# Router logits on two column tiles, and the first expert block's rows gathered in the routing phase

## The reference, cut to what matters

```python
def hierarchical_moe(x, w_rg, b_rg, w_re, b_re, w1, w3, w2):
    p_group = jax.nn.softmax((xf @ w_rg).astype(jnp.float32) + b_rg, axis=-1)
    g_sel = jnp.argmax(p_group, axis=-1)
    e_logits = ((xf @ w_re).astype(jnp.float32) + b_re).reshape(T, N_GROUPS, EXPERTS_PER_GROUP)
    ...
    top_v, top_i = lax.top_k(e_in, TOP_K)
    gate = jax.nn.softmax(top_v, axis=-1) * jnp.take_along_axis(p_group, g_sel[:, None], axis=1)
    ...
    h = jax.nn.silu(lax.ragged_dot(xs, w1, sizes)) * lax.ragged_dot(xs, w3, sizes)
    o = lax.ragged_dot(h, w2, sizes) * gate_s[:, None].astype(x.dtype)
    y = jnp.zeros_like(xf).at[tok_s].add(o)
```

## Time and profile before

| | |
|---|---|
| median of 3 runs | 5463.49 us (5462.31 to 5465.83) |
| the profiled execution itself | 5458.19 us |
| its span | 5456.2 us |
| PE busy | 5086.9 us, 93% of the span |
| DVE busy | 3838.7 us, 70% |
| ACT busy | 2904.5 us, 53% |
| POOL busy | 1286.4 us, 24% |
| mean granted clock of PE | 0.965 |

### The profile page before, as it was taken

The page is one execution under the profiler, slowest core; times in us unless marked ns, Lnnn a source line. Parts: engine busy times, 40 slices in busy tenths (PEclk is TensorE's granted clock), DMA queues, the critical chain, the costliest instruction groups (busy, mean ns, idle before and its releaser), DMA issues. The chain is left out here.

```text
span 5456.2 us, 109973 instructions
## 1 busy us (share of the span) xinstructions
PE 5086.9 (93%) x36030; PEld 4377.2 (80%) x36031; DVE 3838.7 (70%) x6659; ACT 2904.5 (53%) x4913; POOL 1286.4 (24%) x1184
## 2 busy tenths in 40 slices
PE   8999999999999998979999959998999996999994
PEld 6989798988889986868888847888888785888883
DVE  6778887777666668686877747875444556866987
ACT  3343444344388886455756534443777213654765
POOL 2110020000011110054544432200100003543555
PEclk9999999999999998989999979999999997999997
DMA  6776765455499987588998856655545436987997
GB/s 217 216 209 202 207 211 167 125 153 142 140 317 312 316 287 209 162 318 272 330 329 277 282 185 215 224 159 170 166 143 160 131 128 220 326 261 238 364 326 254
DMA packets 755211, 1237.12 MB, mean 227 GB/s; under 512 B 111838, under 2 KB 407277, under 8 KB 754828
## 3 DMA queue, kind: packets, MB, share of 16 engines
q1 hardware_dynamic: 630108, 877.59, 49.4%
q0 software_dynamic: 75312, 286.28, 16.8%
q10 hardware_dynamic: 49408, 68.17, 3.7%
HBM read 917.08 MB, written 333.67 MB: 229 GB/s over the span
## 5 line engine op out<-in xcount | busy, mean ns | idle before, releaser
L622 PE MATMUL qa_ps_out<-qa_x_hi,qa_w_hi 128*128 128x512 f32 x1344 | 529.8, 394 | 23.2 <-DVE qa_w_lo L784 12.9
L622 PE MATMUL qa_ps_out<-qa_x_lo,qa_w_hi 128*128 128x512 f32 x1344 | 525.4, 391 | 0.0
L622 PE MATMUL qa_ps_out<-qa_x_hi,qa_w_lo 128*128 128x512 f32 x1344 | 525.3, 391 | 0.0
L668 ACT ACTIVATE qa_w_hi<-qa_w_whole 128x1024 fp32r<-128x1024 f32 x180 | 191.2, 1062 | 428.7 <-PE qa_ps_out L622 221.7
L622 PE MATMUL qa_ps_out<-qa_w_hi,qa_x_hi 128*128 128x256 f32 x1344 | 381.3, 284 | 0.0
L622 PE MATMUL qa_ps_out<-qa_w_hi,qa_x_lo 128*128 128x256 f32 x1344 | 380.3, 283 | 0.0
L622 PE MATMUL qa_ps_out<-qa_w_lo,qa_x_hi 128*128 128x256 f32 x1344 | 380.3, 283 | 0.0
L2895 DVE CUSTOM_DVE_ANT_0 ga_minus_s<-ga_ps_s,ga_bias 128x512 f32<-128x512 f32 (+1 forms) x256 | 185.4, 725 | 252.7 <-PE ga_ps_s L2831 200.1
L1336 ACT ACTIVATE da_prob<-da_minus_s,da_rows 128x256 f32<-128x256 f32 (+1 forms) x768 | 317.7, 464 | 41.3 <-DVE da_rows L1304 41.3
L1304 DVE CUSTOM_DVE_ANT_0 da_minus_s<-da_ps_s,da_bias 128x256 f32<-128x256 f32 (+1 forms) x768 | 259.9, 375 | 90.4 <-PE da_ps_s L1235 79.3
L622 PEld LDWEIGHTS qa_ps_out<-qa_x_hi,qa_w_hi 128*128 128x128 f32 x1344 | 253.9, 189 | 81.3 <-DVE qa_w_lo L784 17.5
(11 more groups left out here) (523 smaller groups left out, 15475.4 us busy)
## 6 DMA issues: line engine op xcount, KB each, us to landing
a_ex_w_raw<-w SPq DMA_DIRECT2D x128, 1024.0 KB, 8.6
b_ex_w_raw<-w SPq DMA_DIRECT2D x128, 1024.0 KB, 9.4
qa_w_raw<-w_qkv_a SPq DMA_DIRECT2D x144, 512.0 KB, 4.8
a_ex_w_raw<-w POOLq DMA_DIRECT2D x66, 1024.0 KB, 8.6
b_ex_w_raw<-w POOLq DMA_DIRECT2D x66, 1024.0 KB, 8.3
da_q_cross<-qT SPq DMA_DIRECT2D x48, 1024.0 KB, 7.7
da_k_parts<-kT SPq DMA_DIRECT2D x48, 1024.0 KB, 10.1
a_in_o<-o SPq DMA_DIRECT2D x16, 1584.0 KB, 8.0
```

What stands on the lines that cost most here:

```text
L622: done = pe.matmul(out, stationary, moving, start=(k == 0 and i == 0), stop=(k == KH - 1 and i == 2))
L668: act.activation(w_hi[:, p % W_RING], src, ACT.Copy).then_inc(w_hi_done, 1)
```

## The change

Four things change; the rest of the program is the same.
- The logits: `wr` is padded to 64 columns instead of 128, and each of the 8 steps becomes two matmuls, one for tokens 0 to 63 and one for tokens 64 to 127 of the tile, on two column tiles of the array (`tile_position`), writing the upper and the lower 64 partitions of ps_l.
- The first gather: x_row and its semaphore move to `ExpertWeights`, which lives through both phases, and POOL issues the gather of block 0 in the routing phase, after the second entry of its table, once DVE has written `tokens` (new semaphore tokens_kept). The remaining table entries come after it.
- DVE in the routing phase makes `tokens` between the two halves of gate_at; POOL issues the first loads of w2 at its beginning, after waiting for the last load of side 0.
- DVE in the experts phase makes the low part of piece 0 alone ahead of xT_lo, and of pieces 1 to 7 after it.

```diff
-        wr = sb("wr", [P, KC, P])
+        wr = sb("wr", [P, KC, HD])
...
-        ps_l = ps("ps_l", [P, P])
+        ps_l = ps("ps_l", [P, HD])
...
                     for k in range(KC):
-                        done = pe.matmul(ps_l[:], x1T[:, k, :], wr[:, k, :], start=(k == 0), stop=(k == KC - 1))
+                        for side in range(2):
+                            toks = bass.ts(side, HD)
+                            done = pe.matmul(ps_l[toks, :], x1T[:, k, toks], wr[:, k, :], start=(k == 0),
+                                             stop=(k == KC - 1), tile_position=(0, HD * side))
                     done.then_inc(routed, 1)
...
+        self.x_row = ctx.enter_context(nc.sbuf_tensor(f"{tag}_x_row", [P, D], F32))
+        self.x_loaded = sem("x_loaded")
...
                 link(pool.memset(pack[:], 0.0))
+                pool.wait_ge(weights.w13_loaded[W13_PIECES // 2 - 1], 32)
+                for i in range(W2_PIECES // 2):
+                    weights.load_w2(pool, 0, i).then_inc(weights.w2_loaded[i], 16)
                 pool.wait_ge(expert_copied, 1)
...
                 put(routing.PACK, pack[:])
                 put(routing.SIDE, expert_side[:, 1])
+                pool.wait_ge(tokens_kept, 1)
+                pool.indirect_dma_start(out=weights.x_row[:], out_offset=None, in_=scratch.x1,
+                                        in_offset=bass.IndirectOffsetOnAxis(ap=routing.tokens[:, 0:1], axis=0)
+                                        ).then_inc(weights.x_loaded, 16)
                 put(routing.FETCH, fetch[:])
...
-                pool.wait_ge(weights.w13_loaded[W13_PIECES // 2 - 1], 32)
-                for i in range(W2_PIECES // 2):
-                    weights.load_w2(pool, 0, i).then_inc(weights.w2_loaded[i], 16)
...
-                for h in range(2):
+                def mark_gates(h):
...
                 link(dve.memset(place[:, B:B + 1], 0.0))
+                mark_gates(0)
                 dve.wait_ge(inverted, 1)
...
-                link(dve.tensor_copy(routing.tokens[:], place[:]))
+                dve.tensor_copy(routing.tokens[:], place[:]).then_inc(tokens_kept, 1)
+                mark_gates(1)
                 dve.wait_ge(gates_placed, 1)
...
-                split_w13(dve, 0, at.count, 0, range(4), "lo")
+                split_w13(dve, 0, at.count, 0, range(1), "lo")
                 x_parts(0)
-                split_w13(dve, 0, at.count, 0, range(4, DVE_LOWS), "lo")
+                split_w13(dve, 0, at.count, 0, range(1, DVE_LOWS), "lo")
...
-                    if first(b):
-                        pool.indirect_dma_start(out=x_row[:], out_offset=None, in_=scratch.x1,
-                                                in_offset=bass.IndirectOffsetOnAxis(ap=routing.tokens[:, 0:1], axis=0)
-                                                ).then_inc(x_loaded, 16)
-                        pool.sem_inc(picked, 1)
-                        return
...
-                gather_x(0)
+                pool.sem_inc(picked, 1)
```

More of the change, by code:

```diff
@@ L1901, in route_tokens @@
         inverted, gates_marked, gates_placed = sem("inverted"), sem("gates_marked"), sem("gates_placed")
+        tokens_kept = sem("tokens_kept")
         logits = routing.logits
@@ L2300, in experts @@
         w_lo = sb("w_lo", [P, EXPERT_PIECES, D], F32R)
-        x_row = sb("x_row", [P, D])
+        x_row = weights.x_row
         column = sb("column", [P, 1], U32)
@@ L2320, in experts @@
         stepped = sem("stepped")
-        x_loaded = sem("x_loaded")
+        x_loaded = weights.x_loaded
         x_turned = sem("x_turned")
```

## The result

| | before | after |
|---|---|---|
| median | 5464.66 us (6 runs, 5460.20 to 5471.73) | 5433.79 us (6 runs, 5431.86 to 5442.25) |
| the profiled execution | 5458.19 us | 5432.38 us |
| its span | 5456.2 us | 5430.7 us |

The ratio of after to before is 0.9948, with a 95% interval of 0.9938 to 0.9958: some 28 us faster (23 to 34). The two medians are 30.9 us apart. So the sign and the places were right, and a part of the gain was not foreseen.

A forecast was written before the change was run, and what follows sets the result against it. PE, busy in 93% of the span, was taken to bound the kernel. Merges 14.4 us plus starts of the experts 6.6 made 21.0 us saved, forecasting 5442.5 us, with a range of 5434 to 5455.

The forecast's parts named there:

- The group, 1.18 us: PE's logit group in the merges: 32 records at the attention's 0.034 us plus 0.10 for changing tiling, 1.18 instead of 1.70.
- Merges, 14.4 us: Both merges save 14.4 us: 5.0 in layer a, 6.8 in layer b, and 1.3 at each end.
- The ends, 1.3 each: Last two logit groups of each merge: 1.3 us saved per layer, bounds 0.3 and 2.2; route(14) saves 1.2.
- The routing phase, 0.4 later: The routing phase ends 0.4 us later, as PE's ps_gates group must follow the delayed second half of gate_at.
- The start of the experts, 3.3 per layer: PE, freed from waiting for the gather, begins the experts phase 3.3 us earlier per layer, 6.6 in all; bounds 0 and 3.8.
- land within the phase either way: Routing phase: the w2 loads land within it either way and are used only in the next phase.
- covered, by 0.8 us: POOL in the routing phase ends by 2354.6, DVE at 2355.4, so POOL's added work stays hidden by 0.8 us.
- Rival C: More is saved: logit group halved without a tiling price, PE starts experts 3.8 us earlier; 27.1 saved, 5436.4 us; chance 0.14.
- A: Start of the experts does not move, held by PE's table reading or DVE's low parts; 14.4 saved, 5449.1 us; chance 0.14.
- B: In merge a the loop of load and DVE takes all of the 5.0 us; 16.0 saved, 5447.5 us; chance 0.10.
- D: The two tiles' logit matmuls don't run beside each other; group 1.89 us, 1 saved in all, 5462.4 us; chance 0.06.
- E: Slower: a logit record keeps 0.11 us, group 3.6 us in both merges; 54 us more, 5518 us; chance 0.03.

The follow-up runs named there:

- four tiles: The change with the logits on four column tiles of 32 tokens and 40 columns, 64 records in rotation: 5424.1 us, ratio to before 0.9929.
- Tiles in turn: The change with its 16 logit matmuls reordered, all 8 steps on the first column tile, then 8 on the second: 5454.2 us.
- w2 first: The kernel before with only POOL's first two loads of w2 moved to the beginning of the routing phase: 5460.1 us against 5465.8.
- logits alone: The kernel before with the router logits on two column tiles and nothing else: 5453.7 us against 5465.8, ratio 0.9975.

## Why the prediction was right, and where it fell short

- **The group, 1.18 us**: right, from the attention's row. The period of a tile in layer b fell by 0.49, forecast 0.52. By the rule of 60 cycles a matmul (the Trainium skill, TensorEngine Tiling (Array Packing), Instruction Overhead) the edit brings nothing. For tiles in rotation it does not hold: at 2.4 GHz 60 cycles are 0.025 us, and a record of four tiles takes 0.0114. Tiles in turn come out near the prediction's estimate from that page, 0.057 against 0.052, and there the edit indeed brings nothing.
- **Merges, 14.4 us**: 14.9 in this execution. Over all profiles with two tiles in rotation merge a averages 269.5 (six, 267.85 to 270.79) and merge b 240.6, against 275.5 and 248.4 in four with the group of 1.70: 5.9 and 7.8, 13.7 in all. The statement that the loop of load and DVE in layer a gets no faster held: lo(13) starts 211.1 us after the first instruction of the phase, 210.9 before. That loop has a scatter of its own, which the prediction had left out: over the ten profiles with a group of 1.70 us or two tiles in rotation lo(13) starts 210.9 to 214.1 us after it. In the one with four tiles it is 208.8, earlier than in any of them, so for a still faster PE the statement is not shown.
- **The ends, 1.3 each**: 1.10 and 1.07. Both halves of the argument were seen: route(14) gained 1.67, more than the 1.2, and the lower clock of what follows took part of it back.
- **The routing phase, 0.4 later**: 0.20 and 0.09.
- **The start of the experts, 3.3 per layer: this step failed**, and the change came out faster for it. It measured 6.9. The prediction took POOL's first instruction at 2359.28 as the moment when the barrier opens, and bounded the gain by 3.8 from above. PE did begin 0.4 us behind POOL, as that bound says, but POOL's first instruction itself moved by 3.1 us towards DVE's last, from 4.33 to 1.25 us behind it. Two things that the change removes had held it: POOL's drain (2.4 us here, 2.3 per layer by the kernel with w2 first), and the gather's own lead, as a plain instruction starts 0.35 us after the second meeting of the engines (2351.4 to 2351.75) and the gather started 1.0 after it (2358.3 to 2359.28): 0.65 us. All that is left of the gap, from 6.3 to 1.65, goes with the gather, its lead included: 4.7. The rows held a hint: DVE had an idle time of 5.00 put down to POOL's queue, and POOL one of 7.96 put down to issue, though the row of its loads ended at 2351.33.
- **The loads of w2 "land within the phase either way", priced at nothing**: this is the term behind that failure. Before, the last one landed at 2357.5, 2.5 us after DVE's last instruction (2354.95), and the phase ended with it. The step looked at POOL's time to issue them and not at what POOL's drain waits for. The move is worth 2.3 us per layer alone and 5.0 beside the early gather, where the two loads at the end are issued 2.9 us before DVE's last instruction ends, instead of 5.2.
- **POOL in the routing phase, "covered, by 0.8 us"**: it was done 3.2 us ahead of DVE, since its five table instructions took 1.5 us and not 5.0; that too was luck. Its drain, which the step left out, ended 1.7 us ahead of DVE's.
- **What lies behind**: nothing was forecast. Experts of b took 882.8 to 884.0 us in the nine kernels with the early gather, against 885.2 to 887.1 in the three without: some 3 us. Most of it is one place, below.

Rival C had the sign of the surprise and not its cause: it halved the group and put PE 3.8 us earlier. Its 5436.4 is nearer to the 5433.8 measured than the forecast's 5442.5, by luck: the group was not halved, and the bound of 3.8 was the one that fell. That the median lies within 0.2 us of the range is luck too: the step at the experts was off by a factor of two, and the merges alone came out as forecast. Rivals A, B, D and E are out by the rows above.

## What to carry to other kernels

A barrier opens when the last engine has drained. Behind loads that POOL issued, its drain ran up to 6.6 us beyond the row of the issue, until they had landed: put such loads at the beginning of a phase, and look at the drains before taking a phase's end from its last busy engine. In this group of small matmuls fewer moving columns did nothing, while column tiles used in rotation, and four rather than two, made it faster (from 1.70 us to 1.17 and 0.82, with the 0.09 of the longer way in). When a transfer is made earlier, look at what its reader does first: here DVE's new order carried 3.3 of the 4.7 us per layer that the early gather won.

## What the hardware did that I had not expected

A record on four column tiles takes a third of one on two (0.034 to 0.0114), though it has only half the tokens. The starts of the records account for it: twice as many run beside each other in a set, and the sets follow every 0.036 us instead of every 0.058. So a group goes by its 16 sets and hardly by its records; in full proportion a record would have taken a quarter.

And one stretch of DVE's, late in the experts of b. Before, four low parts took 9.80 us, one of them 6.38, and PE waited 1.27 and then 1.25 us (timelines of DVE and PE), 2.5 of the some 3 us above:

```profile
5287.20 9.80 DVE L2496 TENSOR_TENSOR b_ex_w_lo<-b_ex_w_raw,b_ex_w_hi 128x1024 fp32r<-128x1024 f32 x4
...
5297.65 0.66 PE L2464 MATMUL b_ex_ps_h<-ident,b_ex_gate 128*128 128x128 f32 x4 [1.27 <-DVE b_ex_gate L2566]
```

After, the same four, the longest with 3.43:

```profile
5263.83 6.84 DVE L2509 TENSOR_TENSOR b_ex_w_lo<-b_ex_w_raw,b_ex_w_hi 128x1024 fp32r<-128x1024 f32 x4
```

In the kernel before, POOL's indirect DMA of the sums had started 1.67 us after its column was ready, against 0.83 in the change, and the long one of DVE's ran beside POOL's own two low parts. The three kernels with the old start of the experts (before, logits alone, w2 first) show it, the nine with the early gather don't. Why that one issue is late stays open.
